# A large multi-block kernel on one core: the first sixteen modulation columns computed from row tiles, and the bias strips moved between the projections

## The reference, cut to what matters

```python
cond = jax.nn.silu(c)                                   # c: (1, 1024)
mod = (cond @ ada_w[l] + ada_b[l]).reshape(B, 6, D_MODEL)[:, :, None, :]
shift1, scale1, gate1 = mod[:, 0], mod[:, 1], mod[:, 2]
...
u = rmsnorm(x, norm_mix[l]) * (1.0 + scale1) + shift1
aq, ak, av, bq, bkv, biq, bik, biw, cq, ck, cv, g = split_cols(u @ w_in[l])
...
bias = bias_t[:, t5_bucket(dist)]                       # relative position bias, 12 heads
logits = ... * scale + bias[None, :, None]
```

## Time and profile before

| | |
|---|---|
| median of 3 runs | 2829.11 us (2829.11 to 2829.2) |
| profiled execution, its own time | 2827.5 us |
| its span, first to last instruction | 2825.7 us |
| PE busy | 2665.5 us (94%) |
| DVE busy | 1501.7 us (53%) |
| ACT busy | 1108.3 us (39%) |
| mean granted clock of TensorE | 0.966 of full speed |

### The profile page before, as it was taken

One profiled execution on the slowest core, in us unless ns is written; L12 is line 12 of the kernel. 1 busy time (PEld: TensorE's weight loads), 2 busy tenths in 40 slices (PEclk: granted clock), 3 DMA queues, 4 the chain that ended last, 5 costly groups with the idle time before them and its releaser, 6 DMA issues.

```text
span 2825.7 us, 33699 instructions
## 1 busy us (share of the span) xinstructions
PE 2665.5 (94%) x13693; PEld 2199.6 (78%) x13693; DVE 1501.7 (53%) x2577; ACT 1108.3 (39%) x1822; POOL 403.9 (14%) x291
## 2 busy tenths in 40 slices
PE   7999799999999999896899999999999999999998
PEld 6776567878888987784787778889788886888887
DVE  3376867355333269897865553332643753642334
ACT  2446344244332232444355353322542453542223
POOL 0031223110100033441310110000100100111000
PEclk6999899899999999998899999999999999999998
DMA  8343223433333323211342223333231241333331
GB/s 224 100 107 82 71 67 102 121 104 90 97 91 95 98 68 90 67 46 52 89 121 64 57 81 97 96 91 101 65 83 52 81 136 38 91 96 92 95 97 60
DMA packets 482298, 251.31 MB, mean 89 GB/s; under 512 B 14558, under 2 KB 479026, under 8 KB 482143
## 3 DMA queue, kind: packets, MB, share of 16 engines
q1 hardware_dynamic: 479556, 242.49, 30.5%
q0 software_dynamic: 1872, 5.66, 0.7%
q10 hardware_dynamic: 715, 1.01, 0.1%
HBM read 247.00 MB, written 2.13 MB: 88 GB/s over the span
## 4 chain that ended last, share of the span: by engine, by line
PE 77%; DVE 15%; ACT 6%; issue 1%; DMA 0%; POOL 0%; SPq 0%; DVEq 0%; ACTq 0%; POOLq 0%
PE ps L909 18%; PE ps L911 18%; PE ps L913 18%; DVE ps L2377 4%; PE ps L845 2%; PE ps L841 2%; PE ps L843 2%; PE ps L935 2%; PE ps L869 1%; PE ps L1349 1%; PE ps L859 1%; PE ps L861 1%; PE ps L1064 1%; DVE hT L3091 1%; DVE w_r L2244 1%
## 5 line engine op out<-in xcount | busy, mean ns | idle before, releaser
L909 PE MATMUL ps<-XH,wh 128*128 128x512 f32 (+1 forms) x1888 | 766.7, 406 | 13.7 <-ACT arena_f L1679 6.1
L913 PE MATMUL ps<-XH,w_r 128*128 128x512 f32 (+1 forms) x1888 | 751.5, 398 | 4.8 <-DVE w_r L2244 2.9
L911 PE MATMUL ps<-XL,wh 128*128 128x512 f32 (+1 forms) x1768 | 706.8, 400 | 3.3 <-DVE XL L2761 2.8
L2244 DVE TENSOR_TENSOR w_r<-w_f,wh 128x1024 fp32r<-128x1024 f32 (+1 forms) x315 | 377.2, 1200 | 569.9 <-ACT wh L1493 569.8
L1493 ACT ACTIVATE wh<-w_f 128x1024 fp32r<-128x1024 f32 (+2 forms) x406 | 410.4, 1014 | 391.4 <-PE ps L913 214.2
L909 PEld LDWEIGHTS ps<-XH,wh 128*128 128x128 f32 (+1 forms) x1888 | 358.8, 190 | 123.0 <-issue 19.4
L913 PEld LDWEIGHTS ps<-XH,w_r 128*128 128x128 f32 (+1 forms) x1888 | 357.5, 189 | 92.8 <-DVE w_r L2244 5.1
L911 PEld LDWEIGHTS ps<-XL,wh 128*128 128x128 f32 (+1 forms) x1768 | 335.4, 190 | 85.5 <-issue 3.6
L911 PE MATMUL ps<-arena_r,wh 128*128 128x512 f32 (+1 forms) x944 | 349.2, 370 | 4.1 <-DVE arena_r L2485 3.0
L909 PE MATMUL ps<-arena_r,wh 128*128 128x512 f32 (+1 forms) x734 | 271.7, 370 | 21.9 <-ACT arena_r L1520 11.2
L913 PE MATMUL ps<-arena_r,w_r 128*128 128x512 f32 (+1 forms) x734 | 264.6, 360 | 2.7 <-DVE w_r L2244 1.5
(11 more groups left out here) (371 smaller groups left out, 3810.9 us busy)
## 6 DMA issues: line engine op xcount, KB each, us to landing
w_f<-in_mlp_w SPq DMA_DIRECT2D x126, 512.0 KB, 4.1
w_f<-in_w_ff SPq DMA_DIRECT2D x63, 512.0 KB, 4.1
w_f<-in_w_in SPq DMA_DIRECT2D x49, 512.0 KB, 3.9
w_f<-in_ada_w SPq DMA_DIRECT2D x35, 512.0 KB, 4.0
w_f<-in_even_w_in SPq DMA_DIRECT2D x35, 512.0 KB, 3.8
w_f<-in_odd_w_in SPq DMA_DIRECT2D x23, 512.0 KB, 3.8
w_f<-in_even_w_out SPq DMA_DIRECT2D x16, 512.0 KB, 4.0
w_f<-in_xa_w_v SPq DMA_DIRECT2D x16, 512.0 KB, 4.2
```

What stands on the lines that cost most here:

```text
L909: e.matmul(b, hi[:, k, :], xh, start=u.first and k == 0, stop=False)
L911: e.matmul(b, hi[:, k, :], xl, start=False, stop=False)
L913: last = e.matmul(b, lo[:, k, :], xh, start=False, stop=u.final and k == u.kc - 1)
L2244: e.tensor_tensor(flat(u, 1), flat(u, 0), high_flat(u).bitcast(F32), ALU.subtract).then_inc(dve.sem, dve.up("low", u.n))
```

## The change

The sixteen column units are replaced by sixteen row units ("mod"): unit 2k + h holds the 128 rows of chunk k and the 1024 columns of half h (h = 0 is shift1, h = 1 is scale1). Each is again 512 KB, now 4 KB in one piece on each partition. For the chunks k = 2 and 3 PE multiplies the tile directly, sixteen products with one column each (`mod_rows`); for the other six chunks DVE multiplies the 128x1024 tile with a scalar per partition and accumulates (`mod_sum`), one instruction per unit. PE then sums the two accumulated tiles over the partitions with sixteen products with ones. All twelve strips are turned over between the projections: two after the first part, one after each of the other ten.

```diff
+MOD_ROWS = (2, 3)
...
-    plans = {"ada first": ada[:16]}
+    plans = {"mod": [Unit("mod", 2 * k + h, [A["ada_w"][0][k * P:(k + 1) * P, h * D:(h + 1) * D]], split=False)
+                     for k in range(KC) for h in range(2)]}
...
+            def mod_rows(b, i):
+
+                k = MOD_ROWS[i]
+                for h in range(2):
+                    u = mods[2 * k + h]
+                    w.wait_ge(d_raw[u.raw], "unit", u.n)
+                    w.wait_ge(dve, "cond")
+                    for j in range(KC):
+                        at = i * 16 + h * KC + j
+                        last = e.matmul(b[:, at:at + 1], flat(u, 0)[:, j * P:(j + 1) * P], cond[:, k, :], start=True, stop=True)
+                last.then_inc(pe.sem, pe.up("mod rows", i))
...
+            rows_bank, freed = lin.take("mod rows")
+            w.wait_ge(*freed)
+            mod_rows(rows_bank, 0)
             rms_sums("mix", KC)
...
+            mod_rows(rows_bank, 1)
+            b, freed = lin.take("mod")
             w.wait_ge(*freed)
-            for u in first:
-                ada_first(u, ada_bank)
-
-            for h in range(4):
-                flip_over(h)
+            for h in range(2):
+                w.wait_ge(dve, "mod sum", 2 * (KC - 1) + h)
+                for j in range(KC):
+                    last = e.matmul(b[:, h * KC + j:h * KC + j + 1], mod_sums[h][:, j * P:(j + 1) * P], ones[:, 0:1],
+                                    start=True, stop=True)
+            last.then_inc(pe.sem, pe.up("mod"))
+
             for i, part in enumerate(plans["project parts"]):
                 run_units(part)
-                if i < 8:
-                    flip_over(4 + i)
+                for h in (i + 1,) if i else (0, 1):
+                    flip_over(h)
...
-            for u in plans["ada first"]:
+            for u in mods:
                 round_ahead(u.n)
-            for h in range(4):
-                flip_out(h)
-
...
+            def mod_sum(k):
+
+                for h in range(2):
+                    u = mods[2 * k + h]
+                    w.wait_ge(d_raw[u.raw], "unit", u.n)
+                    w.wait_ge(dve, "cond")
+                    if k == 0:
+                        e.tensor_scalar(mod_sums[h], flat(u, 0), cond[:, k, :], None, ALU.mult).then_inc(
+                            dve.sem, dve.up("mod sum", u.m))
+                    else:
+                        w.wait_ge(dve, summed[h])
+                        e.scalar_tensor_tensor(out=mod_sums[h], in0=flat(u, 0), scalar=cond[:, k, :], in1=mod_sums[h],
+                                               op0=ALU.mult, op1=ALU.add).then_inc(dve.sem, dve.up("mod sum", u.m))
+                    summed[h] = dve.count
+
+            summed = [0, 0]
+            mod_sum(0)
             for n in range(1, 5):
                 turn_pack(n)
+            mod_sum(1)
             for k in range(KC):
                 add_square("mix", k)
...
+            for k in range(2, KC):
+                if k not in MOD_ROWS:
+                    mod_sum(k)
+            b, mod = lin.of("mod rows"), modc[:, 0:16]
+            w.wait_ge(pe, "mod rows", 1)
+            w.wait_ge(dve, "vec", 0)
+            e.tensor_tensor(mod, b[:, 0:16], columns("ada_b", 0, 16), ALU.add).then_inc(dve.sem, dve.up("mod bias"))
+            w.wait_ge(dve, "mod bias")
+            e.tensor_tensor(mod, b[:, 16:32], mod, ALU.add).then_inc(dve.sem, dve.up("mod part"))
+            lin.free(dve, "mod rows")
+            for u in mods:
                 lower_ahead(u.n)
-                if u.m % 2 == 0:
-                    ada_sum(u)
...
+            w.wait_ge(dve, "mod part")
+            w.wait_ge(pe, "mod")
+            e.tensor_tensor(mod, lin.of("mod")[:, 0:16], mod, ALU.add).then_inc(dve.sem, dve.up("mod", 15))
+            lin.free(dve, "mod")
```

More of the change, by code:

```diff
@@ L385, in plan @@
             us[-1].raw = RAW_SLOTS
-    for j, u in enumerate(plans["ada first"][:len(ADA_PLACES)]):
+    for j, u in enumerate(plans["mod"][:len(ADA_PLACES)]):
         u.raw = RAW_SLOTS + 1 + j
@@ L590, in program @@
         ws_rows = Ring("ws rows", ws_bufs, rings, after=ws_index)
-        of_ada = lambda u: "pe" if u.m >= ADA_LATE or (u.m < 16 and u.m % 2) else "dve"
+        of_ada = lambda u: "pe" if u.m >= ADA_LATE else "dve"
+        mods = plans["mod"]
+        mod_sums = [a[:, 2:4, :].rearrange("p a b -> p (a b)") for a in (ws, PT)]
         tiles = [(h, qt) for h in range(HEADS) for qt in range(NT)]
@@ L774, in sync_program @@
                     old = u.raw_before
-                    if old.name == "ada" and of_ada(old) == "dve":
+                    if old.name == "mod":
+                        w.wait_ge(dve, "mod sum", old.m)
+                    elif old.name == "ada" and of_ada(old) == "dve":
                         w.wait_ge(dve, "ada sum", old.m)
@@ L936, in ada_column @@
                 last.then_inc(pe.sem, pe.up("unit", u.n))
-            def ada_first(u, b):
-                if u.m % 2 == 0:
[L941 to L944, removed]
+            def mod_rows(b, i):
[8 more added lines that the diff above has]
+                last.then_inc(pe.sem, pe.up("mod rows", i))
             late_bank = [None]
@@ L1042, in flip_over @@
                 e.matmul(b[:, :], flip, flips[h % NT], start=True, stop=True).then_inc(pe.sem, pe.up("flip", h))
-            first = iter(plans["ada first"])
-            ada_bank, freed = lin.take("ada first")
+            mod_rows(rows_bank, 1)
+            b, freed = lin.take("mod")
             w.wait_ge(*freed)
-            for u in first:
-                ada_first(u, ada_bank)
-            for h in range(4):
-                flip_over(h)
+            for h in range(2):
[4 more added lines that the diff above has]
+            last.then_inc(pe.sem, pe.up("mod"))
             for i, part in enumerate(plans["project parts"]):
                 run_units(part)
-                if i < 8:
-                    flip_over(4 + i)
+                for h in (i + 1,) if i else (0, 1):
+                    flip_over(h)
             flush()
@@ L1753, in scalar_program @@
                 run_steps(part)
-                if i < 8:
-                    flip_out(4 + i)
+                for h in (i + 1,) if i else (0, 1):
+                    flip_out(h)
             flush()
@@ L2528, in vector_program @@
             e.tensor_scalar(ct, ct, 0.5, None, ALU.mult).then_inc(dve.sem, dve.up("cond"))
+            e.memset(lamb[BUCKETS:BUCKETS + 1, 0:12], 1.0).then_inc(dve.sem, dve.up("table row"))
+            def mod_sum(k):
[11 more added lines that the diff above has]
+                    summed[h] = dve.count
@@ L2529, in vector_program @@
+            summed = [0, 0]
+            mod_sum(0)
             for n in range(1, 5):
                 turn_pack(n)
+            mod_sum(1)
             for k in range(KC):
                 add_square("mix", k)
-            e.memset(lamb[BUCKETS:BUCKETS + 1, 0:12], 1.0).then_inc(dve.sem, dve.up("table row"))
-            def ada_first(u):
-                lower_ahead(u.n)
-                if u.m % 2 == 0:
-                    ada_sum(u)
-            for u in plans["ada first"]:
-                ada_first(u)
```

## The result

| | before | changed |
|---|---|---|
| median | 2829.15 us (2829.11 to 2831.35, 4 runs) | 2810.11 us (2809.64 to 2813.38, 4 runs) |
| profiled execution, its span | 2825.7 us | 2807.9 us |

The account below looks back on a forecast made before the run. PE was taken as the bound, busy 94% of the span, its one-column rounds paced by weight loads. Terms -22.8 + 3.6 + 0.8 = -18.4 us took the median 2829.1 to 2810.7 us, range 2804 to 2818.

Parts of the forecast that it names:

- The first product 22.8 us earlier (49.2): End of modulation on PE and handover: the first projection product comes at 49.2 instead of 72.0, 22.8 us earlier.
- The transfers: Loads of the row tiles: 1.26 us a tile at the rate of x, the sixteenth landing at 34.8 instead of 44.1.
- The first rival: Row-tile loads keep the old rate, 1.81 us a tile; first product at 54.2, gain 13.4, total 2815.7 us; chance 0.12.
- DVE's products: DVE's multiply-and-add on row tiles of 1024 columns in the modulation: 1.27 us each, between 1.2 and 1.4.
- The first group at half clock: PE's first `mod_rows`, 32 instructions from 22.2: 6.9 us at clock 0.50, ending at 29.1 at the latest.
- the rival with the clock high: PE's one-column products run at clock 1.00, DVE becomes the bound; gain 24.3, total 2804.8 us; chance 0.08.
- Four strips, +3.6: Four strips moved in between the projections, where PE has no idle time: 0.89 us each, 3.6 us given back.
- The clock, +0.8: Projections start at clock 0.50 until it rises: 0.8 us lost, between 0 and 1.5, partly covered by PE's waits.
- Sum: Whole kernel: -22.8 + 3.6 + 0.8 = -18.4 us, from a median of 2829.1 to 2810.7 us; chance 0.66.
- Slow projections: Rival: projections run at clock 0.50 because no dense strips raised it first; in full 2876 us; chance 0.05.
- Given back later: Rival: the projections run into something at a fixed time and the gain is lost, 2829 us; chance 0.04.

Follow-up runs that it names:

- e4_both_ahead: The changed kernel with PE's second group of one-column products (`mod_rows`) also placed ahead of the sum of squares; 2811.18 us, ratio 0.9935.
- e5_chunk1_behind: The changed kernel with DVE's two products of chunk 1 moved behind the additions of squares; 2811.76 us, ratio 0.9925.
- e6_all_on_dve: The changed kernel with no chunks multiplied directly by PE, DVE doing all sixteen tiles; 2815.47 us, ratio 0.9942.
- e3_pieces_512: The changed kernel with each row tile fetched as eight 512-byte pieces per partition, every second 128-column block; 2814.92 us, ratio 0.9951.
- e1_strips_only: The kernel before with only the four strips moved between the projections, modulation still by columns; 2832.54 us, ratio 1.0009.
- e2_rows_only: The changed kernel with the strip move undone, so four strips stay ahead of the projections; 2814.37 us, ratio 0.995.
- e8_dense_both: e4_both_ahead plus four dense 128x512 products, results overwritten, before the sum with ones and four behind it; 2811.81 us, ratio 0.993.
- e9_dense_behind_sum: e4_both_ahead plus two dense 128x512 products, results overwritten, behind the sum with ones; 2811.67 us, ratio 0.9933.
- e11_dense_both_again: The same kernel as e8_dense_both, run and profiled once more; 2811.1 us, ratio 0.9923.
- a0_changed_again: The changed kernel, unedited, run and profiled a second time on another occasion for comparison; 2814.66 us, ratio 0.9939.
- e7_dense_before_sum: e4_both_ahead plus five dense 128x512 products, results overwritten, before the sum with ones; 2812.51 us, ratio 0.9936.

## Why the prediction was right, step by step

**The first product 22.8 us earlier (49.2).** It was 21.6 (50.41). The mechanism stands: PE's chain sets the end (`e4_both_ahead`, `e5_chunk1_behind` shorten it from either side), with groups of 6.98 and 6.96 us where 6.9 were said. The missing 1.2 us lie ahead of and behind it: the 32 transposes of x took 6.08 us where they had taken 4.99, so DVE's additions started at 24.61 and not at 23.6; and the handover took 48.23 to 50.41, 2.2 for 2.0. The transposes varied from 4.99 to 6.48 us over the fourteen profiles, at a granted clock of 1.00; `e6_all_on_dve` has 4.99 and the changed kernel again 6.48. What sets them wasn't found.

**The transfers.** 1.26 us a tile and the sixteenth landed near 34.8 were forecast; the rows show 402 to 414 GB/s, and the last issue at 19.5 with 15.1 to 15.5 us to landing gives about 35. `e3_pieces_512` shows that the way a row is cut into pieces decides. The first rival put the first product 5.0 us later (54.2 against 49.2); with such pieces it was 3.4 later (53.78 against 50.41).

**DVE's products** at 1024 columns: 6.06 / 5 = 1.21 us back to back against 1.27, at the low end of 1.2 to 1.4.

**The first group at half clock.** I let it end at 29.1 "at the latest". It took 3.64 us, at full clock, and it made no difference, since PE then waited for DVE until 30.21. That is also what became of the rival with the clock high: it was so for one group of three, the one that is off the path.

**Four strips, +3.6.** From the first part's copy to the last unit's copy it was 64.77 us before and is 67.39: 2.62 for three strips, 0.87 each, and 0.9 for the fourth behind it. Right, and `e1_strips_only` with `e2_rows_only` shows both sides of that account.

**The clock, +0.8.** Here the working was off. The first part took 12.42 us before and 12.46 now, at a clock that rose only 3.4 us in (at 53.8, where I had said about 52): +0.04. I had seen PE wait for `XH` and `XL`, but put it down as a partial cover. It is the bound: DVE makes one chunk of `XL` each 1.45 us, and the eight take the same time in every profile. First and last rows of them, before and changed:

```profile
71.91 0.75 DVE L2569 SCALAR_TENSOR_TENSOR XL<-sq,modc,XH 128x512 fp32r<-128x512 f32 x1 [4.45 <-ACT XH L1746]
80.61 1.63 DVE L2569 SCALAR_TENSOR_TENSOR XL<-sq,modc,XH 128x512 fp32r<-128x512 f32 x2
```

```profile
50.30 0.75 DVE L2605 SCALAR_TENSOR_TENSOR XL<-sq,modc,XH 128x512 fp32r<-128x512 f32 x1
59.01 1.63 DVE L2605 SCALAR_TENSOR_TENSOR XL<-sq,modc,XH 128x512 fp32r<-128x512 f32 x2
```

From the first start to the last end it is 10.33 and 10.34 us, and the copy of the result begins 2.20 and 2.23 us after that. In the other profiles this remainder is 2.19 when the clock was up at once or soon (`e8_dense_both`, `e9_dense_behind_sum`), 2.45 in the second profile of the changed kernel (up after 3.8 us), 3.13 in `e1_strips_only` (5.2) and 3.44 in `e4_both_ahead` (6.1). So here a late clock cost nothing at 3.4 us, and 1.25 us at 6.1: the range of 0 to 1.5 held, the value taken was too high. The exception is `e11_dense_both_again` with 4.28, where the dense products held PE up while DVE went ahead.

**Sum.** -21.6 + 3.5 + 0.04 = -18.1 against -18.03 in the profiles and -19.0 in the medians; the first term was off by 1.2 us and the clock's by 0.8, with opposite signs. That the sum fits better than its terms is luck. So is the closeness of 19.0: the second five executions of the changed kernel (`a0_changed_again`) are 15.3 us below the kernel before by the medians, 17 by the ratio. What is shown is a gain of 0.5 to 0.8% (the two intervals together), and the mechanism behind it; a term of 1 us can be checked in a profile only, not in the median.

**Rivals.** Slow projections: refuted, the clock rose within 6.2 us of the first product in every profile. Given back later: not in the changed kernel (+0.3 us over 2675.9). It did show, as 4 to 6 us, in six profiles of other kernels (`e1_strips_only`, `e5_chunk1_behind`, `e7_dense_before_sum`, `e8_dense_both` and its repetition, `e9_dense_behind_sum`), in none of the two of the changed kernel. In the stretches shown above it goes with a lower granted clock; its cause stays open.

## What to carry to other kernels

A product of a big matrix with one vector is paid on PE by the tile, not by the column, and it does not bring the clock up (34.3 us of it ran at 0.50 from end to end): fetch it by rows in pieces of 4 KB and let DVE accumulate whole rows, so that PE only sums over partitions once. Before a term is priced for PE, look at which engine paces that stretch; if another one does, a slow PE is free up to its slack. And take a profile of the same kernel twice before a difference of a few microseconds is put down to an edit.

## What the runs showed of the hardware

- Pieces of 512 bytes with gaps between them moved at 290 GB/s and pieces of 4 KB at 402 to 414, with as many bytes, the same rows and the same queue, in the same stretch of the program.
- One-column float32 products cost 0.114 us an instruction at 1.00 and 0.217 at 0.50. In `e4_both_ahead` the clock fell while 64 of them ran; right after dense work had raised it, 32 ran at 1.00 throughout (`e8_dense_both` and `e7_dense_before_sum`, 3.63 us), but not in the repetition of the former (4.34 us).
- The clock rose 2.9 to 6.2 us after dense work began, and the same program had its falls and rises at different times in two executions, which lay 6.9 us apart at the first softmax row. Its fastest and slowest of ten executions lay 11 us apart.
